# Second feed-forward block of a macaron layer: first feature block computed directly, token sums in place on VectorE, modulation on ScalarE, a buffer of its own for the second weight unit

## Chip, cores and metric

The kernel runs on one core of a Trainium2 chip. The metric is the device time of one execution in microseconds; times below are of this kernel on that one core, and the profile is of one execution.

## The reference, cut to what matters

One layer on 1024 latent tokens of width 1024 (and a context of 256): a feed-forward block, a mixer, a second feed-forward block, a last norm. The change touches the second feed-forward block alone.

```python
def rmsnorm(x, g):
    y = x * lax.rsqrt(jnp.mean(x * x, axis=-1, keepdims=True) + EPS)
    return y * g

def modulate(h, shift, scale):
    return h * (1 + scale) + shift

def swiglu(h, w1, w2):                       # w1: 1024 x 5632, w2: 2816 x 1024
    gate, up = jnp.split(h @ w1, 2, axis=-1)
    return (jax.nn.silu(gate) * up) @ w2

...
x = x + m_x[5] * (jnp.concatenate([ret_x, gm_x], axis=-1) @ w_out[l])      # the mixer's output projection
x = x + 0.5 * m_x[8] * swiglu(modulate(rmsnorm(x, norm_g[l, 2]), m_x[6], m_x[7]), ffn2_w1[l], ffn2_w2[l])
return rmsnorm(x, final_g)
```

## The kernel before

Everything lies transposed: features on the 128 partitions, tokens along the free axis, in two halves of TB = 512 tokens. Each float32 product is made of three matmuls on split operands: a *high* part (ScalarE copies the float32 tile to float32r) and a *low* part (tile minus high, on GpSimd or VectorE); high x high, high x low, low x high (`mm3`, L1449 to L1451, and `product`, L1702 to L1704).

The five engines each have a program written out by hand, in order; semaphores join them. Nothing schedules them: what stands ahead in an engine's program runs first. SyncE issues all loads.

**The second feed-forward block** goes through NF = 22 feature blocks of 128 hidden features, with two units of weights each: `block_unit(g)`, 1 MB into WR slot 0 (gate and up columns, 1024 x 256), and `down_unit(g)`, 0.5 MB into W2R. The product of a feature block's weights with all tokens is a 2x2 block product (feature rows 0 to 511 and 512 to 1023, by gate and up, by the token halves), computed by Strassen's scheme in its form by Winograd with NM = 7 products instead of 8. It needs sums of weight blocks (`weight_sums`: four VectorE subtractions and additions, L1193 to L1199, one of them in place in WR) and four sums of token blocks, made once: V0 = B12 - B11, V1 = B22 - V0, V2 = B22 - B12, V3 = B21 - V1, where B11, B21 are the modulated tiles of the first token half and B12, B22 those of the second. The product m of block g waits for the low part of its weights and adds up in PSUM (`product_bank`); ScalarE copies three of the banks to SBUF (PU, U2, U3: `first_copy`, `second_copy`, `third_copy`), VectorE adds the other bank to them, ScalarE takes SiLU, VectorE multiplies, and the result is split into PXH and PXL. The down projection (`down`, 8 output tiles for each token half, 48 matmuls) goes through four PSUM banks, from which VectorE adds into X (L1355). It runs one block late: the down projection of block g-1 stands between the products of block g. `block_period` is one such period on each engine; the last 20 periods are a loop and its tail.

**The order around the change.** The mixer's output projection ends with eight fills of 24 matmuls for the second token half (`("out", 1, b)`). Meanwhile VectorE adds them into X (L1302), ScalarE squares (L657), VectorE adds the squares (L920) and makes the weight sums of block 0; ScalarE and GpSimd split the weights of block 0 (`weight_high`, L720, `weight_low`, L597). TensorE then runs products 0 and 1 of blocks 0 and 1, which need only the first token half, with the two norm steps of the second half in between (`norm_sum`, L1459; `norm_scale`, L1469). For the second half, VectorE does for each k of four: two scalings by the norm factor (`scaled`, L948, into B12 and B22), two modulations (`modulated`, L955), V0 and V1 (L1389, L1392). ScalarE makes the high parts (`token_high`, L746), GpSimd the low parts of V1, V2 and V3 (`token_low`, L608), VectorE those of V0 and of B22 itself (L1397, L1406). V0 and V2 share one buffer, V1 and V3 another (VT0, VT1). So block 0 has its products 2 to 6 behind those token sums; block 1's weights go through the same WR slot as block 0's and are loaded when block 0's low parts are done.

## Time and profile before

| | |
|---|---|
| runs | 2225.57, 2230.71, 2232.66 us; median 2230.71 |
| profiled execution | 2225.84 us, of which the span from first to last instruction is 2224.0 |
| mean granted TensorE clock | 0.984 of full speed |
| TensorE / VectorE / GpSimd / ScalarE busy | 96% / 59% / 30% / 24% of the span |
| end of the mixer's output projection | 1488.0 us |
| start of the first down projection of the second feed-forward block | 1557.2 us |
| one period of the loop behind it | 30.1 us |

Rows are read like this: a row of a timeline gives start and length in us, the engine, the line of the kernel, the operation with output<-inputs, and in brackets how long the engine stood idle before it and who released it. A row of groups gives count, busy time, the mean in ns and the idle time before. PE is TensorE, DVE VectorE, ACT ScalarE, POOL GpSimd, SPq SyncE's queue. A matmul of 512 columns shows 0.39 us but the next one starts 0.23 us after it: they overlap.

### The profile page before, as it was taken

What the parts mean: (1) busy time and instruction counts of PE and PEld (TensorE: products, weight loads), DVE (VectorE), ACT (ScalarE), POOL (GpSimd) and SP (SyncE); (2) the same over time, 40 slices, a digit from 0 to 9 for tenths busy, and PEclk for the clock granted to TensorE, in tenths of its full rate; (3) what the DMA queues carried; (4) which work ended last, traced back from release to release, by engine and by line L of the source; (5) the groups of instructions that cost most, each with busy time, mean ns of one, the idle gap of its engine ahead of it and who ended that gap; (6) DMA issues with size and microseconds to landing.
All of it is one profiled execution on the core that took longest, in us unless ns stands there. A gap on an engine that the chain in (4) does not pass through costs nothing.

```text
span 2224.0 us, 28807 instructions
## 1 busy us (share of the span) xinstructions
PE 2142.8 (96%) x10884; PEld 1793.8 (81%) x10884; DVE 1320.5 (59%) x2012; ACT 539.5 (24%) x812; POOL 664.3 (30%) x349
## 2 busy tenths in 40 slices
PE   7999999999999999998999999995999999999995
PEld 3688888888888888887888898874888888888884
DVE  4654454454454454469644444478777777777767
ACT  3312111111111111124221222334222323223222
POOL 1611111111111111126232232565343443343430
PEclk9999999999999999999999999997999999999997
DMA  9212112112111111113101021210101111111112
GB/s 343 76 48 94 54 40 85 56 47 74 67 47 67 74 47 66 76 38 120 57 20 38 20 88 55 76 67 29 57 30 54 57 57 57 57 39 46 57 38 76
DMA packets 28376, 144.41 MB, mean 65 GB/s; under 512 B 3360, under 2 KB 4640, under 8 KB 15008
## 3 DMA queue, kind: packets, MB, share of 16 engines
q1 hardware_dynamic: 28320, 143.64, 17.4%
q8 instruction: 38, 0.62, 0.1%
q14 instruction: 18, 0.15, 0.0%
HBM read 139.44 MB, written 4.19 MB: 65 GB/s over the span
## 4 chain that ended last, share of the span: by engine, by line
PE 87%; DVE 6%; issue 2%; DMA 2%; POOL 1%; ACT 1%; SPq 0%; DVEq 0%; ACTq 0%; POOLq 0%
PE PS L1449 22%; PE PS L1451 21%; PE PS L1450 21%; PE PS L1702 6%; PE PS L1703 6%; PE PS L1704 6%; PE PS L1495 1%; DVE ACC L920 1%; PE PS L1486 1%; POOL HL L510 1%; DMA WR<-w_units 1%; DMA X<-x 1%; PE PS L1644 1%; DVE B L955 1%; DVE HF L955 1%
## 5 line engine op out<-in xcount | busy, mean ns | idle before, releaser
L1449 PE MATMUL PS<-HH,WH 128*128 128x512 f32 x1088 | 427.0, 393 | 3.7 <-POOL HL L510 3.0
L1450 PE MATMUL PS<-HL,WH 128*128 128x512 f32 x1088 | 424.1, 390 | 0.0
L1451 PE MATMUL PS<-HH,WL 128*128 128x512 f32 x1088 | 423.9, 390 | 0.0
L493 POOL TENSOR_TENSOR WL<-WR,WH 128x2048 fp32r<-128x2048 f32 x42 | 193.3, 4603 | 535.1 <-ACT WH L643 534.9
L1355 DVE SCALAR_TENSOR_TENSOR X<-PS,GATE,X 128x512 f32<-128x512 f32 x352 | 242.9, 745 | 93.6 <-PE PS L1451 93.6
L1449 PEld LDWEIGHTS PS<-HH,WH 128*128 128x128 f32 x1088 | 204.7, 188 | 46.6 <-issue 4.1
L1451 PEld LDWEIGHTS PS<-HH,WL 128*128 128x128 f32 x1088 | 204.7, 188 | 42.9
L1450 PEld LDWEIGHTS PS<-HL,WH 128*128 128x128 f32 x1088 | 204.8, 188 | 41.8 <-issue 0.7
L1078 DVE TENSOR_TENSOR PR<-SG,PS 128x512 f32<-128x512 f32 (+1 forms) x66 | 39.5, 599 | 296.8 <-ACT SG L695 291.5
L597 POOL TENSOR_TENSOR WVL<-WR,WVH 128x512 fp32r<-128x512 f32 x88 | 124.4, 1424 | 255.0 <-ACT WVH L720 255.0
L1094 DVE SCALAR_TENSOR_TENSOR X<-PS,GATE,X 128x512 f32<-128x512 f32 x176 | 132.1, 751 | 108.0 <-PE PS L1451 108.0
L695 ACT ACTIVATE SG<-PS 128x512 f32<-128x512 f32 (+1 forms) x66 | 34.5, 523 | 641.3 <-PE PS L1451 641.2
L1449 PE MATMUL PS<-PH,W2H 128*128 128x512 f32 (+1 forms) x528 | 188.4, 357 | 0.6 <-DVE X L1094 0.6
L1451 PE MATMUL PS<-PH,W2L 128*128 128x512 f32 (+1 forms) x528 | 187.0, 354 | 0.0
L1450 PE MATMUL PS<-PL,W2H 128*128 128x512 f32 (+1 forms) x528 | 186.8, 354 | 0.0
L526 POOL TENSOR_TENSOR W2L<-W2R,W2H 128x1024 fp32r<-128x1024 f32 x22 | 53.6, 2438 | 375.1 <-ACT W2H L704 375.1
L1054 DVE SCALAR_TENSOR_TENSOR AS<-WR,CS,AS 128x256 f32<-128x256 f32 x336 | 156.4, 539 | 0.0
L1449 PE MATMUL PS<-PXH,W2H 128*128 128x512 f32 x352 | 140.1, 398 | 2.8 <-DVE PXL L1349 1.4
L1702 PE MATMUL PS<-HH,WVH 128*128 128x512 f32 x352 | 139.7, 397 | 2.1 <-POOL WVL L597 1.4
L1703 PE MATMUL PS<-HL,WVH 128*128 128x512 f32 x352 | 139.2, 396 | 0.0
L1451 PE MATMUL PS<-PXH,W2L 128*128 128x512 f32 x352 | 138.6, 394 | 0.0
L1704 PE MATMUL PS<-HH,WVL 128*128 128x512 f32 x352 | 138.1, 392 | 0.0
...
## 6 DMA issues: line engine op xcount, KB each, us to landing
...
```

The source lines that it names most:

```text
L493: pool.tensor_tensor(WL[:, slot], WR[:, slot], WH[:, slot].bitcast(F32), ALU.subtract).then_inc(s_lo[slot], 1)
L526: pool.tensor_tensor(w2l[:, j], w2r[:, :], w2h[:, j].bitcast(F32), ALU.subtract).then_inc(s_w2lo, 1)
L597: pool.tensor_tensor(WVL[:, m], weight_block(m), WVH[:, m].bitcast(F32), ALU.subtract).then_inc(s_wl, 1)
L1054: ins = dve.scalar_tensor_tensor(dst, w, c, dst, ALU.mult, ALU.add)
L1094: dve.scalar_tensor_tensor(xv, PS[down_bank(s, k)][:, 0:nt], GATE[:, 0, k, s:s + 1], xv, ALU.mult, ALU.add).then_inc(s_yd, 1)
L1355: dve.scalar_tensor_tensor(xv, y_bank(n)[:, :], GATE[:, 2, d, 0:1], xv, ALU.mult, ALU.add).then_inc(s_fyd, 1)
L1449: pe.matmul(dst, wh, xh, start=first, stop=False)
L1450: pe.matmul(dst, wh, xl, start=False, stop=False)
L1451: return pe.matmul(dst, wl, xh, start=False, stop=last)
L1702: pe.matmul(bank[:, :], wh, xh, start=first, stop=False, skip_group_check=True)
L1703: pe.matmul(bank[:, :], wh, xl, start=False, stop=False, skip_group_check=True)
L1704: ins = pe.matmul(bank[:, :], wl, xh, start=False, stop=k == 3, skip_group_check=True)
```

## The change

1. **Block 0 is computed directly**: gate and up of each token half as plain sums over all eight feature tiles, 4 x 24 matmuls (`direct`), so that it needs no token sums and no weight sums. Its gate and up land in banks of their own (0 and 1 for the first half, 2 and 3 for the second); VectorE multiplies SiLU(gate) by up straight out of PSUM. Products 2 to 6 of block 1 are now the first that need token sums.
2. **Weights of block 1** have a buffer of their own, RAW1, loaded once the mixer's inputs are done; the weight sums ahead of the norm are those of block 1. Their parts go to seven slots in another order (`SLOT1`), since block 0 takes four.
3. **Token sums in place** in B11, B12, B21, B22 (V0 in B11, V1 in B22, V2 in B12, V3 in B21); all their low parts are made by VectorE. GpSimd makes the low parts of B12 instead (`norm_low`).
4. **Modulation** of the second half is one ScalarE instruction (`second_modulated`, a scale and a bias per partition) instead of VectorE's.
5. TensorE runs, after the output projection: direct first half (48 matmuls, with the norm steps between), products 0 and 1 of block 1, direct second half (48), products 2 and 3 of block 1, down projection of block 0's first half, product 4, second half, products 5 and 6. Then the loop, unchanged, from block 2 on.

```diff
@@ TensorE @@
+            def direct(bank, t, n, done=None, ready=None, base=0):
+                slot, half = DIRECT[n], n % 2
+                cols = slice(t * TB, (t + 1) * TB)
+                pe.wait_ge(s_wl, n + 1)
+                for k in range(4):
+                    if ready is not None:
+                        pe.wait_ge(ready, base + k + 1)
+                    ins = mm3(PS[bank][:, :], WVH[:, slot, k, :], WVL[:, slot, k, :], HH[:, 4 * half + k, cols],
+                              HL[:, 4 * half + k, cols], half == 0 and k == 0, half == 1 and k == 3)
...
-            product(0, 0, 0)
+            direct(A0, 0, 0, s_m[0])
             norm_sum(2, 2)
-            product(0, 0, 1)
+            direct(A0, 0, 1, s_m[1])
             norm_scale(2, 2)
+            direct(B_, 0, 2)
+            direct(B_, 0, 3, s_m[5])
             product(1, 1, 0)
-            pe.wait_ge(s_c11, 1)
+            pe.wait_ge(s_g1, 1)
             product(1, 1, 1)
...
+            direct(2, 1, 0, s_m[2], s_hl, 8 * J[2, 2])
+            direct(3, 1, 2, s_m[4])
+            direct(2, 1, 1, s_m[6], s_bl)
+            direct(3, 1, 3, s_m[3])
+            pe.wait_ge(s_p1, 1)
+            product(1, 1, 2, s_vl[1])
...
+            product(1, 1, 3, s_vl[0])
+            pe.wait_ge(s_fp[1], 1)
             pe.wait_ge(s_fyd, NYB)
-            block_period(0, 0, first=True)
-            block_period(1, 1, second=True)
+            down(0, 0)
+            pe.wait_ge(s_u2, 1)
+            product(1, 1, 4, s_vl[2])
+            down(0, 1)
+            pe.wait_ge(s_u3, 1)
+            product(1, 1, 5, s_vl[3])
+            pe.wait_ge(s_c22, 1)
+            product(1, 1, 6)
@@ VectorE @@
+            for k in range(KT):
+                scaled(2, 2, k)
...
+                dve.tensor_tensor(B11[:, k, :], B12[:, k, :], B11[:, k, :], ALU.subtract).then_inc(s_v[0], 1)
...
+            dve.tensor_tensor(PU[:, 0, :], SG1[:, :], PS[A0][:, :], ALU.mult).then_inc(s_fp[0], 1)
...
+            for k in range(4):
+                dve.wait_ge(s_v[3], k + 1)
+                token_low(1, k)
+            for k in range(4):
+                token_low(0, k)
...
+            for d in range(KT):
+                down(0, 0, d)
+                if d % 2:
+                    token_low(3, d // 2)
             up_first(1, 1)
+            next_sums(2)
+            for d in range(KT):
+                down(0, 1, d)
+                if d == 1:
+                    gate_second(1)
@@ ScalarE @@
+            def second_modulated(k):
+                j, h = J[2, 2], modulated_tile(2, 2, k)
+                act.wait_ge(s_xm, 8 * j + k + 1)
+                act.activation(h, h, ACT.Identity, scale=GAIN[:, 2, k, 0:1], bias=MODS[:, 6 * KT + k, 0:1]).then_inc(s_hf, 1)
@@ GpSimd @@
+            for n, slot in enumerate(DIRECT):
+                low_part(slot, weight_block(slot), n + 1)
+            for m in range(3):
+                weight_low(1, m, RAW1)
             norm_rsqrt(2, 2)
-            weight_low(1, 0)
-            weight_low(1, 1)
-            for v in (1, 2, 3):
-                for k in range(4):
-                    token_low(v, k)
-            block_period(0, first=True)
-            block_period(1)
+            norm_low(2, 2, 0, 4)
+            for m in range(3, NM):
+                weight_low(1, m, RAW1)
+            down_low(0)
+            for m in range(6):
+                weight_low(2, m)
+            down_low(1)
@@ SyncE @@
+            sp.wait_ge(s_cat, 16)
+            sp.dma_start(RAW1[:, :, :], w_units[U_FFN2 + 1]).then_inc(s_raw1, 16)
...
-            block_unit(1)
-            with sp.Fori(1, NF - 1) as g:
+            block_unit(2)
+            sp.wait_ge(s_dl, 1)
+            down_unit(1)
+            with sp.Fori(2, NF - 1) as g:
```

**VectorE's order, before**: the last of the four rounds on the second half and what follows (X is the residual, PS4 the bank with the norm factor, VT0 and VT1 the buffers of the sums, L1323 the addition into PU).

```order
L948 TENSOR_TENSOR B12_147<-X_49,PS4 128x512
L948 TENSOR_TENSOR B22_148<-X_49,PS4 128x512
L955 TENSOR_SCALAR B12_147<-B12_147,GAIN_57,MODS_55 128x512 [waits scaled_done]
L955 TENSOR_SCALAR B22_148<-B22_148,GAIN_57,MODS_55 128x512 [waits scaled_done]
L1389 TENSOR_TENSOR VT0_139<-B12_147,B11_145 128x512 [waits modulated_done]
L1392 TENSOR_TENSOR VT1_140<-B22_148,VT0_139 128x512 [waits token_sum0_ready,modulated_done]
L1323 TENSOR_TENSOR PU_134<-PU_134,PS1 128x512 [waits first_product_copied,product1_ready]
L1397 TENSOR_TENSOR HL_51<-VT0_139,HH_50 128x512 [waits token_sum0_high_done]
L1400 TENSOR_TENSOR VT0_139<-B22_148,B12_147 128x512 [waits token_sum1_ready,token_sum0_low_done]
```

**VectorE's order, changed**, the same place: the scalings stand together, the modulations are gone, the gated multiply (L1458) and block 6's low part (L1462) stand ahead of the sums, and the low parts of V1 and V0 (L1446) come after all sums.

```order
L1011 TENSOR_TENSOR B12_142<-X_49,PS4 128x512 x3
L1011 TENSOR_TENSOR B22_144<-X_49,PS4 128x512 x4
L1455 TENSOR_TENSOR B11_141<-B12_142,B11_141 128x512 [waits modulated_done,modulated_low_done]
L1455 TENSOR_TENSOR B11_141<-B12_142,B11_141 128x512 [waits modulated_done] x3
L1458 TENSOR_TENSOR PU_134<-SG1_128,PS0 128x512 [waits product1_ready,silu_first_half_done]
L1462 TENSOR_TENSOR HL_51<-B22_144,HH_50 128x512 [waits modulated_high_done] x4
L1466 TENSOR_TENSOR B12_142<-B22_144,B12_142 128x512 [waits token_sum0_ready,modulated_low_done] x4
L1470 TENSOR_TENSOR B22_144<-B22_144,B11_141 128x512 [waits last_block_low_done,token_sum2_ready] x4
L1418 TENSOR_TENSOR PXL_133<-PU_134,PXH_132 128x512 [waits gated_high_done0]
L1474 TENSOR_TENSOR B21_143<-B21_143,B22_144 128x512 [waits token_sum1_ready] x4
L1446 TENSOR_TENSOR V2L_146<-B22_144,V2H_145 128x512 [waits token_sum1_high_done,token_sum3_ready] x4
```

Behind the eleven rows come the low parts of V0 and V2 and the first additions of the down projection; before, the sums of each k stood right behind its modulation.

**ScalarE's order, before**, around the first SiLU of the block (G2, SG1):

```order
L737 ACTIVATE U3_131<-PS0 128x512 [waits product4_ready]
L720 ACTIVATE WVH_141<-ST_127 128x512 [waits weight_sums_ready,block_unit_loaded,product2_ready]
L720 ACTIVATE WVH_141<-WR_52 128x512 [waits weight_sums_ready,block_unit_loaded,product3_ready]
L720 ACTIVATE WVH_141<-ST_127 128x512 [waits weight_sums_ready,block_unit_loaded,product4_ready]
L770 ACT_TABLE_LOAD
L770 ACTIVATE G2_135<-G2_135 128x512 [waits gate_second_half_ready]
L774 ACTIVATE SG1_128<-PS0 128x512 [waits product5_ready]
L720 ACTIVATE WVH_141<-WR_52 128x512 [waits block_unit_loaded,product5_ready]
```

**ScalarE's order, changed**, from the norm high parts of the second half on; SG1 is the SiLU of block 0's first half, V2H the high part of sum V1.

```order
L678 ACTIVATE HH_50<-B12_142 128x512 [waits modulated_done] x4
L772 ACT_TABLE_LOAD
L772 ACTIVATE SG1_128<-PS1 128x512 [waits product5_ready]
L894 ACTIVATE B22_144<-B22_144,MODS_55,GAIN_57 128x512 [waits scaled_done] x4
L678 ACTIVATE HH_50<-B22_144 128x512 [waits modulated_done] x4
L749 ACTIVATE PU_134<-PS7 128x512 [waits product0_ready]
L762 ACTIVATE PXH_132<-PU_134 128x512 [waits gated_ready0]
L776 ACTIVATE W2H_137<-W2R_129 128x1024 [waits down_unit_loaded]
L731 ACTIVATE WVH_139<-RAW1_151 128x512 [waits weight_sums_ready,product2_ready]
L731 ACTIVATE WVH_139<-ST_127 128x512 [waits weight_sums_ready,product4_ready]
L766 ACTIVATE V2H_145<-B22_144 128x512 [waits token_sum1_ready] x4
L766 ACTIVATE HH_50<-B11_141 128x512 [waits token_sum0_ready] x4
```

The table load and the first SiLU moved up between the two groups of modulations (L894), and the high parts of the token sums (L766) stand behind two weight parts that wait for products of the direct block.

**GpSimd's order, before**, from the norm's reciprocal root on (VXL: low parts of token sums):

```order
L499 TENSOR_TENSOR RS_66<-MS_65,NEGH_67 128x4 [waits norm_mean_ready]
L597 TENSOR_TENSOR WVL_142<-WR_52,WVH_141 128x512 [waits weight_block_high_done] x2
L608 TENSOR_TENSOR VXL_144<-VT1_140,VXH_143 128x512 [waits token_sum1_high_done] x4
L608 TENSOR_TENSOR VXL_144<-VT0_139,VXH_143 128x512 [waits token_sum2_high_done] x4
L608 TENSOR_TENSOR VXL_144<-VT1_140,VXH_143 128x512 [waits last_block_low_done,token_sum3_high_done] x4
L597 TENSOR_TENSOR WVL_142<-ST_127,WVH_141 128x512 [waits weight_block_high_done]
L597 TENSOR_TENSOR WVL_142<-WR_52,WVH_141 128x512 [waits weight_block_high_done]
```

**GpSimd's order, changed**, from the same place (RAW1: block 1's own unit):

```order
L518 TENSOR_TENSOR RS_66<-MS_65,NEGH_67 128x4 [waits norm_mean_ready]
L529 TENSOR_TENSOR HL_51<-B12_142,HH_50 128x512 [waits modulated_high_done] x4
L616 TENSOR_TENSOR WVL_140<-RAW1_151,WVH_139 128x512 [waits weight_block_high_done]
L616 TENSOR_TENSOR WVL_140<-ST_127,WVH_139 128x512 [waits weight_block_high_done]
L616 TENSOR_TENSOR WVL_140<-RAW1_151,WVH_139 128x512 [waits weight_block_high_done]
L616 TENSOR_TENSOR WVL_140<-ST_127,WVH_139 128x512 [waits weight_block_high_done]
L623 TENSOR_TENSOR W2L_138<-W2R_129,W2H_137 128x1024 [waits down_unit_high_done]
L616 TENSOR_TENSOR WVL_140<-WR_52,WVH_139 128x512 [waits weight_block_high_done] x2
```

Twelve low parts of token sums left the engine, four of B12 came, and the weight parts of block 1 and W2L follow at once.

## Rows read from the trace of the kernel before

**Rows 1.** Page, part 2: busy tenths of TensorE in 40 slices of the span

```profile
PE   7999999999999999998999999995999999999995
```

**Rows 2.** Stretches: us, length, busy us per engine (x instructions), PEclk, DMA

```profile
1503.20:1517.40 14.20, 5.05 (x13) 2.96 (x13) 13.82 (x21) 3.45 (x6) 4.15 (x3) 0.68 0.00 1
...
1526.40:1532.30 5.90, 0.01 (x1) 0.01 (x1) 5.90 (x6) 2.37 (x4) 4.43 (x3) 0.71 0.00 0
...
1552.70:1573.60 20.90, 20.86 (x85) 17.05 (x85) 16.59 (x22) 5.60 (x9) 8.58 (x7) 0.92 0.00 1
...
1573.60:1603.70 30.10, 30.10 (x132) 24.59 (x131) 22.61 (x28) 8.95 (x15) 12.00 (x9) 1.00 0.14 53
```

**Rows 3.** Waits, 1480 to 1580 us: who for whom, total, times, longest

```profile
PE PS L1702 <- POOL VXL L608: 9.9, 4, 3.2
...
PE PS L1702 <- ACT U L733: 6.3, 1, 6.3
...
PE PS L1702 <- ACT U L737: 5.9, 1, 5.9
...
PE PS L1702 <- POOL WVL L597: 1.4, 1, 1.4
```

**Rows 4.** Groups, TensorE, 1603 to 2130 us: count, busy us, mean ns, idle before

```profile
L1702 PE MATMUL PS<-VXH,WVH 128*128 128x512 f32 x209 | 82.0, 392 | 0.3 <-ACT U L733 0.3
```

**Rows 5.** Timeline, TensorE: start, length (us), line, output<-inputs, [idle before <-releaser]

```profile
1491.37 1.05 PE L1459 MATMUL PS<-ONES,ACC 128*128 128x1 f32 x8 [0.47 <-DVE ACC L920]
...
1495.13 1.02 PE L1469 MATMUL PS<-DG,ONES 128*128 128x512 f32 x2
...
1603.93 0.40 PE L1702 MATMUL PS<-HH,WVH 128*128 128x512 f32 x1
```

**Rows 6.** Timeline, VectorE, around the norm of the second half

```profile
1488.20 0.75 DVE L1302 SCALAR_TENSOR_TENSOR X<-PS,GATE,X 128x512 f32<-128x512 f32 x1 [4.09 <-PE PS L1451]
...
1496.19 1.29 DVE L948 TENSOR_TENSOR B<-X,PS 128x512 f32<-128x512 f32 x2 [0.17 <-PE PS L1469]
```

**Rows 7.** Timeline, VectorE and GpSimd, single rows between 1496 and 1575 us

```profile
1558.07 5.51 DVE L1355 SCALAR_TENSOR_TENSOR X<-PS,GATE,X 128x512 f32<-128x512 f32 x8 [2.06 <-PE PS L1451]
...
1572.66 2.48 DVE L1349 TENSOR_TENSOR PXL<-PU,PXH 128x512 fp32r<-128x512 f32 x1
...
1496.20 2.55 POOL L597 TENSOR_TENSOR WVL<-WR,WVH 128x512 fp32r<-128x512 f32 x2 [2.49 <-ACT WVH L720]
...
1572.19 2.41 POOL L601 TENSOR_TENSOR W2L<-W2R,W2H 128x1024 fp32r<-128x1024 f32 x1 [4.13 <-ACT W2H L780]
```

**Rows 8.** Timeline of ScalarE; then its groups: count, busy us, mean ns, idle

```profile
1481.03 1.14 ACT L720 ACTIVATE WVH<-WR 128x512 fp32r<-128x512 f32 x2
...
L770 ACT ACT_TABLE_LOAD x1 | 1.3, 1283 | 0.0
...
L831 ACT ACTIVATE KZ<-PS,Z 128x512 f32<-128x512 f32 x16 | 9.7, 698 | 0.0
```

**Rows 9.** Timeline, GpSimd and VectorE side by side, 1518 to 1526 us

```profile
1518.84 6.53 POOL L608 TENSOR_TENSOR VXL<-VT,VXH 128x512 fp32r<-128x512 f32 x4 [2.93 <-ACT VXH L746]
...
1520.85 1.67 DVE L1400 TENSOR_TENSOR VT<-B,B 128x512 f32<-128x512 f32 x1
1522.44 1.79 DVE L1403 TENSOR_TENSOR VT<-B,VT 128x512 f32<-128x512 f32 x1
```

**Rows 10.** Timeline, SyncE's queue and VectorE: a load and its first reader

```profile
1545.81 0.34 SPq L456 DMA_DIRECT2D WR<-w_units  x1
...
1551.06 0.69 DVE L1193 TENSOR_TENSOR ST<-WR 128x512 f32<-128x512 f32 x1 [3.82 <-DMA WR<-w_units]
```

**Rows 11.** Timeline, TensorE, start-up of the second feed-forward block

```profile
1511.48 0.79 PE L1702 MATMUL PS<-VXH,WVH 128*128 128x512 f32 x1 [3.19 <-POOL VXL L608]
...
1520.82 0.63 PE L1704 MATMUL PS<-HH,WVL 128*128 128x512 f32 x1
1521.25 0.63 PE L1702 MATMUL PS<-HH,WVH 128*128 128x512 f32 x1
```

366 lines of the change are left out of this document (204 added, 162 removed).

## Prediction

> **What bounds the kernel now.** The page comes first: TensorE's row of tenths stands at 9 nearly everywhere and has one dip away from the two ends, a 5 in slice 28, which begins at 27 x 55.6 = 1501 us [rows 1]. The table of stretches opens that dip. From 1573.7 us on, one feature block takes 30.10 us, TensorE is busy throughout, and 132 matmuls went by, 0.228 us each, at a granted clock of 1.00. From 1503.2 to 1517.4 it passes 13 matmuls in 14.2 us at a clock of 0.68, and from 1526.4 to 1532.3 one [rows 2]. The waits of the stretch name what it stood for: 9.9 us for GpSimd's low parts of the token sums (L608) and once each 6.3 and 5.9 us for ScalarE's copies U2 and U3 [rows 3]. The time to win is therefore the start-up of the second feed-forward block, between the last output projection (1488.0) and the steady loop; the loop itself has no idle TensorE time (0.3 us in 527 us) [rows 4] and its code is unchanged.
>
> Call the mark "end of block 2" the last matmul of product 6 of the third feature block, at 1603.9 in the trace (the first matmul after it starts at 1603.93) [rows 5]. Everything behind it runs at TensorE's pace, so the kernel gains what this mark moves.
>
> **TensorE's own work.** Before the mark it does 132 x 3 less one projection of 48, so 348 matmuls; the direct block has 2 x 2 x 8 x 3 = 96 instead of 84, so 360 afterwards: 12 x 0.228 = +2.7 us. With 360 x 0.228 = 82.1 us and 2.5 us for the two norm steps (0.47 of waiting and 1.05, then 1.0) [rows 5] the mark could not come before 1488.0 + 84.6 = 1572.6. The bound of the gain is 31.3 us. The rest of the sum is how much of it the new waits keep.
>
> **Durations taken.** VectorE on 128x512: 0.60 us start to start (two take 1.28) [rows 6], 0.68 for an addition into X (eight take 5.51) [rows 7]. ScalarE 0.52 start to start (two take 1.14) [rows 8]; GpSimd 1.26 (two take 2.55), and 2.41 for W2L [rows 7]. What one engine writes is taken up by the next within 0.1 us.
>
> **VectorE and GpSimd get in each other's way.** While GpSimd works through four low parts without a pause (6.53 us, 1.63 each), VectorE's subtractions show 1.67 and 1.79 instead of 0.68 [rows 9], and so I charge 1.0 us to a VectorE instruction with two SBUF operands that finds GpSimd running, and 2.1 us against W2L from its start (half a microsecond later, a subtraction took 2.48 there) [rows 7]. Instructions that read PSUM are not charged (the scalings and the additions into X, [rows 6, 7]). The change puts all sixteen low parts of the token sums on VectorE, twelve more than now, while GpSimd splits weights beside it, so this decides the sum. The Trainium skill, page "SBUF — State Buffer", section "Who interferes with whom", puts it harder: the pair of ports is locked for the whole instruction and the second one blocks fully. By the letter of that, an alternating pair would cost 1.29 + 0.68 = 1.97 us; the trace has 1.63. The row is used; the rule's reading is a rival below.
>
> **The chain after the change.** *1488.0 to 1517.9.* TensorE has 96 direct matmuls and products 0 and 1 of block 1 (24), 27.4 us, and the norm steps, with no wait. Its weights are there: the four direct parts stand two fills earlier in ScalarE's queue than now, and block 1's unit has a buffer of its own, loaded while the mixer's output is projected, so that the wait for a weight low part ahead of block 1 (1.4 us) goes [rows 3]. The scale row is ready at 1496.2 as now, VectorE scales eight tiles to 1501.0, ScalarE modulates behind it. For this ScalarE step on 128x512 no row exists: a plain copy takes 0.62 (1.14 less 0.52), a scaled one from PSUM 0.70 [rows 8]; either leaves it 0.8 us or less away from where it is counted and off the path, I take 0.70. The table load for SiLU (1.28 [rows 8]) now stands before product 1: SG1 is ready near 1503.6, TensorE asks at 1504.3, so it costs nothing, with 0.7 us of cover. The low parts of the second half's first tiles are there by 1506, asked at 1507.0; those of the last four by 1509.5, asked at 1512.4.
>
> *1517.9 to 1526.7: the first new wait.* Product 2 needs the low parts of token sum 1. VectorE's order is: 8 scalings (1501.0), 4 sums V0 of which three meet GpSimd's norm low parts (+3, 1506.4), the gated multiply, 4 low parts of block 6 (1509.4), 4 sums V2 and 4 sums V1, one meeting GpSimd each (+2, 1516.3), one low part, 4 sums V3 (1519.3). Then come the four low parts wanted; they meet weight low parts 5 and 6 and then W2L (+1.0, +1.0, +2.1), because ScalarE hands those over just then: finished at 1520.0, 1521.6, 1523.2 and 1525.9. TensorE waits 2.2 + 0.8 + 0.8 + 1.9 = 5.7 us and is through product 2 at 1526.7, through product 3 at 1529.5.
>
> *To 1536.7: projection of block 0, first half.* VectorE still has 4 low parts, a multiply, 4 low parts and one more before its first addition at 1531.8; its 8 additions carry 4 low parts between them. With four PSUM banks TensorE's fifth and seventh pieces wait: 0.4 + 1.2 = 1.6 us. Product 4 ends at 1539.5.
>
> *To 1553.5: second half.* VectorE now does the addition into PU and four weight sums (0.73 each, dependent) ahead of the additions: the fifth piece waits to 1544.5, 2.3 us, another 0.5 behind it. Products 5 and 6 end at 1553.5.
>
> *Block 2.* Products 0 to 3 end at 1564.6. Product 4 needs U2, which stands on ScalarE behind the first weight part of block 3, and that behind its load. SyncE issues the load only after W2L of block 1 (POOL: five weight parts and W2L after 1551.6, so 1561.7). In the trace its first reader starts 5.25 us after its issue (1545.81 to 1551.06) [rows 10]; so 1567.3, two highs and a copy, 1569.1: a wait of 4.5 us, where the trace of before has 6.3 [rows 3]. The remaining 84 matmuls end at 1588.4.
>
> **Sum.** 1603.9 - 1588.4 = 15.5 us earlier. Against it stands the clock. In the trace the matmuls went 0.43 us apart (the 1.2 GHz level) after the interrupted stretch, from 1511.5 to 1521.6, then 0.23 again (2.4 GHz) [rows 11]; after the wait of 6.3 us it was eight matmuls, 8 x 0.2 = 1.6 us. I charge 1.6 us behind the wait of 4.5 us, and 1.0 us for product 3, most of whose delay the projection's waits absorb. Gain: 15.5 - 2.6 = 12.9, taken as 13 us. Nothing else is charged: VectorE's and GpSimd's collisions before 1488 (four lows against the weight sums, up to 4 us) fall into VectorE's 4.1 us of idle time before 1488.2 [rows 6]; if that cover fails, the norm step slips by as much, 2 us for 2.
>
> The profiled execution took 2225.84 us (span 2224.0): 2212.8. The three runs have their median at 2230.71, 4.9 us above it, so the forecast is put at 2217.7, 2217.5 rounded.
>
> **Rivals.**
> *Harder collisions or a slower clock (2222).* If GpSimd and VectorE exclude each other for whole instructions (1.29 and 0.68), the first wait becomes about 10 us instead of 5.7 and the mark 1595.1: gain 8.8. If instead the low clock level lasts from product 2 to the end of the first half projection (36 matmuls more at +0.2 = 7 us, less absorbed waits), the mark is 1595.5: gain 8.4. For: the trace kept the low level for 22 matmuls after an interrupted stretch much like the new one. Against: GpSimd's instructions alternate at 1.63 [rows 9].
> *No collisions (2207).* If VectorE's order falls between GpSimd's instructions, all the charges (7 us and what follows from them) go: mark 1579.5, gain 24. Against: both engines are fed by the same ScalarE queue in turn.
> *The new order is ScalarE's problem; the change gives little (2228).* Behind its waits for products 2 and 4 (L731) stand the token highs; if each of the in-order steps slips by what the modulations and the table load add (8 x 0.1 + 1.3) at the three places where TensorE waits already, and the norm step slips by 4 us from the uncovered collisions, some 10 us go: gain 3.
> *Slower.* One mechanism: the clock. The new start has waits of 0.4 to 4.5 us spread over 1518 to 1569. If they keep TensorE at 1.2 GHz from product 2 on, its 156 matmuls up to block 2's product 4 take 0.427 each; the waits vanish behind them, product 4 starts at 1588.7 and the mark is 1609.8, 6 us later than now; if it lasts through block 2, 1624.6, +21 us, 2251. It decides from block 2's product 4 on; below it the change is not slower. Against: in the trace dense work was granted the full clock again each time, as from 1552.7 on (0.92, then 1.00) [rows 2].
>
> **Chances.** Forecast 0.64, its own range 2212 to 2222; harder collisions or clock 0.17; none 0.09; little 0.06; slower 0.04. A measurement of this kernel tells about 0.3%, 6.7 us, from no change. The forecast counts as faster but for its tail, the second case for two thirds, the third wholly: faster 0.79, within 0.3% 0.17, slower 0.04. The range 2208 to 2226 leaves out most of "none", half of "little" and "slower", and allows for the 3.5 us by which the runs differ.
>
> **What would show it.** Right: direct matmuls from 1488 to 1518 with no wait; then a wait on VectorE's V2L lasting 5 to 7 us in pieces at product 2; waits on X additions of 1 to 3 us in each half projection; one wait on U2 of 4 to 5 us in block 2; VectorE subtractions of 1.7 us beside GpSimd's. Block 2 ends near 1591. Wrong: a wait on SG1 or on a low part of HL before 1518; no wait at product 2; a granted clock under 0.8 after 1530; a period other than 30.1 us in the loop.

## Result and profile after

The changed kernel takes 2218.25 us (median of 5 runs, 2215.21 to 2220.49); the kernel before took 2228.82 in the same comparison (5 runs, 2225.57 to 2232.66). The ratio is 0.995 with a 95% interval of 0.9937 to 0.9964, so 10.6 us are gained (8.0 to 14.0 by the interval), where 13 were forecast. Three executions of the kernels below, or of the kernel before beside them, took 3584 to 6221 us and are left out of every median. The profiled execution took 2215.21 us with a span of 2213.4; before it was 2225.84 and 2224.0.

The page of the changed kernel, part 2, TensorE's tenths and its granted clock:

```profile
PE   8899999999999999998999999998899999999995
...
PEclk9999999999999999999999999999999999999998
```

The 5 in slice 28 [rows 1] is gone; two 8s stand in slices 28 and 29. The stretches show what is left (start:end, length, TensorE's busy us and matmuls, clock, DMA):

```profile
1503.20:1518.00 14.80, 14.80 (x66) 1.00 0.00 1
1518.00:1527.00 9.00, 5.80 (x23) 0.95 0.00 1
1527.00:1540.00 13.00, 9.42 (x31) 0.77 0.13 42
1540.00:1555.00 15.00, 13.45 (x58) 1.00 0.00 0
1555.00:1570.00 15.00, 12.29 (x53) 1.00 0.28 103
1570.00:1590.00 20.00, 16.80 (x65) 0.83 0.01 2
1590.00:1620.10 30.10, 30.10 (x133) 1.00 0.14 53
```

From 1503 to 1518 TensorE has no gap, where it had passed 13 matmuls in 14.2 us [rows 2]. Three places remain: 1518 to 1527, 1527 to 1540, 1570 to 1590. The waits from 1480 to 1580 us name them:

```profile
PE PS L1789 <- ACT U L753: 5.7, 1, 5.7
...
PE PS L1536 <- POOL W2L L623: 3.6, 1, 3.6
...
PE PS L1789 <- issue: 2.3, 1, 2.3
PE PS L1536 <- DVE X L1424: 1.6, 2, 1.3
...
PE PS L1789 <- DVE V2L L1446: 0.9, 1, 0.9
...
PE PS L1546 <- DVE ACC L983: 0.6, 1, 0.6
```

The 9.9, 6.3, 5.9 and 1.4 us of [rows 3] have become 5.7, 3.6, 2.3, 1.6 and 0.9. The same waits in TensorE's timeline, and the mark:

```profile
1491.90 0.27 PE L1546 MATMUL PS<-ONES,ACC 128*128 128x1 f32 x1 [0.59 <-DVE ACC L983]
...
1519.56 0.47 PE L1789 MATMUL PS<-V2H,WVH 128*128 128x512 f32 x1 [0.88 <-DVE V2L L1446]
...
1524.86 0.47 PE L1789 MATMUL PS<-HH,WVH 128*128 128x512 f32 x1 [2.32 <-issue]
...
1532.86 0.70 PE L1536 MATMUL PS<-PXH,W2H 128*128 128x512 f32 x1 [3.58 <-POOL W2L L623]
...
1573.20 0.79 PE L1789 MATMUL PS<-V3H,WVH 128*128 128x512 f32 x1 [5.66 <-ACT U L753]
...
1594.38 0.39 PE L1789 MATMUL PS<-HH,WVH 128*128 128x512 f32 x1
```

**The length of the start-up** is used from here on: from the first matmul of the norm sum to the first behind the mark. It was 1491.37 to 1603.93 [rows 5], 112.6 us; now it is 1491.90 to 1594.38, 102.5 us, for twelve matmuls more. Counting TensorE's matmuls from start to start splits it: at 0.229 us each they need 79.2 us before and 82.0 now; gaps over 0.5 us add 27.6 and 16.4; matmuls 0.33 to 0.5 us apart (36 and 26 of them) add 6.3 and 4.9, of which 28 and 23, with 5.4 and 4.6 us, go at about 0.43 us, the slow clock level, and the rest are single ones 0.34 us apart behind a wait; rounding takes 0.6 and 0.8 off. So the start-up gains 10.1 us: 11.2 of gaps and 1.4 of these matmuls, less 2.7 for more work. It begins 0.5 us later, and from the mark to the end of the span it took 620.1 us before and 619.0 here. That 1.1 us is no part of the change: the eleven kernels of the table below have the same loop but for the exchanged loads, and ten of their traces show 619.0 to 620.7 there, one (GpSimd asks later) 613.8. So the 10.6 us of span are 10.1 of start-up and 1.1 behind it, less the 0.5 ahead.

**Where the low parts got stuck.** Product 3 (1524.86) is put down to "issue", but it begins as GpSimd's weight low part of its slot ends. GpSimd's timeline (start, length, [idle before]):

```profile
1511.87 12.89 POOL L616 TENSOR_TENSOR WVL<-RAW,WVH 128x512 fp32r<-128x512 f32 x1 [4.45 <-ACT WVH L731]
1524.72 1.75 POOL L616 TENSOR_TENSOR WVL<-ST,WVH 128x512 fp32r<-128x512 f32 x1
...
1529.81 2.79 POOL L623 TENSOR_TENSOR W2L<-W2R,W2H 128x1024 fp32r<-128x1024 f32 x1
```

An instruction of 1.3 us took 12.89. VectorE meanwhile:

```profile
1501.51 6.46 DVE L1455 TENSOR_TENSOR B<-B,B 128x512 f32<-128x512 f32 x4
...
1510.90 2.49 DVE L1466 TENSOR_TENSOR B<-B,B 128x512 f32<-128x512 f32 x4
1513.31 2.49 DVE L1470 TENSOR_TENSOR B<-B,B 128x512 f32<-128x512 f32 x4
...
1518.72 2.50 DVE L1446 TENSOR_TENSOR V2L<-B,V2H 128x512 fp32r<-128x512 f32 x4
1521.13 2.50 DVE L1446 TENSOR_TENSOR HL<-B,HH 128x512 fp32r<-128x512 f32 x4
1523.54 0.69 DVE L1482 TENSOR_TENSOR UP<-G,PS 128x512 f32<-128x512 f32 x1
1524.13 6.26 DVE L1446 TENSOR_TENSOR V3L<-B,V3H 128x512 fp32r<-128x512 f32 x4
```

Nineteen VectorE instructions with two SBUF operands start 0.60 us apart while GpSimd's stands (the last at 1522.93); then one with an operand in PSUM (L1482) comes, and GpSimd is done 1.2 us after its start. Ahead of that, and behind it, the two alternate: four take 6.46 and 6.26 us, 1.6 each, as in [rows 9].

### The profile page after: what moved, and what is told of

Same layout as the page of the kernel before. It is cut to its first block, busy times and chain, and to the rows that moved or that the text cites. A ratio compares the mean times of both kernels' runs of the same rounds, so it can differ in the third digit from the quotient of the medians.

```text
span 2213.4 us, 28764 instructions
## 1 busy us (share of the span) xinstructions
PE 2140.8 (97%) x10896; PEld 1792.3 (81%) x10896; DVE 1315.8 (59%) x2009; ACT 544.0 (25%) x818; POOL 665.6 (30%) x338
## 4 chain that ended last, share of the span: by engine, by line
PE 88%; DVE 5%; POOL 2%; DMA 1%; issue 1%; ACT 1%; SPq 0%; DVEq 0%; POOLq 0%; ACTq 0%
PE PS L1536 22%; PE PS L1538 22%; PE PS L1537 21%; PE PS L1789 6%; PE PS L1790 6%; PE PS L1791 6%; PE PS L1582 2%; POOL WVL L616 1%; DMA WS<-ada_units 1%; PE PS L1573 1%; POOL HL L529 1%; PE PS L1731 1%; DVE DG L996 1%; DVE ACC L983 1%; DMA WR<-w_units 1%
## 5 line engine op out<-in xcount | busy, mean ns | idle before, releaser
L1537 PE MATMUL PS<-PXL,W2H 128*128 128x512 f32 x352 | 138.8, 394 | 0.0
L1789 PE MATMUL PS<-HH,WVH 128*128 128x512 f32 x336 | 132.4, 394 | 2.3 <-issue 2.3
L1790 PE MATMUL PS<-HL,WVH 128*128 128x512 f32 x336 | 132.3, 394 | 0.0
```

The costliest lines, as they stand in the source:

```text
L1537: pe.matmul(dst, wh, xl, start=False, stop=False)
L1789: pe.matmul(bank[:, :], wh, xh, start=first, stop=False, skip_group_check=True)
L1790: pe.matmul(bank[:, :], wh, xl, start=False, stop=False, skip_group_check=True)
```

## Experiments

All ratios and gains are to the kernel before as it ran beside each kernel: median 2228.82 us beside the changed one; 2227.11 beside "pauses", "second weights early" and "loads exchanged"; 2228.64 beside "one pause", "both" and the exchange in the kernel before; 2229.23 beside the last three. The gain is the difference of the two medians. Since the changed kernel ran beside none of the others, gains are compared here and not medians. "Start-up" is the length defined above, in the profiled execution, one of each kernel.

| kernel | median us | gain us | ratio, 95% | start-up us |
|---|---|---|---|---|
| before | 2228.82 | | | 112.6 |
| changed | 2218.25 | 10.6 | 0.995 (0.9937 to 0.9964) | 102.5 |
| loads exchanged, in the kernel before | 2223.32 | 5.3 | 0.9971 (0.996 to 0.9983) | 108.9 |
| pauses in VectorE | 2218.18 | 8.9 | 0.996 (0.9948 to 0.9972) | 103.8 |
| one pause | 2217.31 | 11.3 | 0.9943 (0.9926 to 0.996) | 102.5 |
| second weights early | 2214.60 | 12.5 | 0.9945 (0.9933 to 0.9958) | 101.1 |
| loads exchanged | 2209.65 | 17.5 | 0.9925 (0.9911 to 0.9939) | 96.1 |
| both | 2211.72 | 16.9 | 0.9914 (0.9897 to 0.9931) | 95.2 |
| GpSimd asks later | 2215.45 | 13.8 | 0.9941 (0.9922 to 0.9959) | 101.4 |
| modulation on VectorE | 2217.60 | 11.6 | 0.995 (0.9938 to 0.9963) | 104.8 |
| V1's low parts on GpSimd | 2218.25 | 11.0 | 0.9953 (0.994 to 0.9965) | 105.9 |

No run undoes the direct block, the buffer RAW1 or the sums in place by themselves. That the direct block and the buffer fill the hole from 1503 to 1518 is read from the waits that are gone there; how the gain divides between them was not tested.

### Pauses in VectorE's run

Does VectorE's unbroken run keep GpSimd out? Each of its sums V2, V1 and V3 and of the low parts of V0, V1 and V2 waits for the one before it; the wait is met by the program's order and leaves only a gap.

```diff
+                dve.wait_ge(s_v[2], k)          # ahead of V2's k-th sum; the like for V1, V3 and the low parts of V0, V1, V2
```

> The changed kernel with one kind of wait more: each of VectorE's sums V2, V1, V3 and each low part of the token sums waits for the one before it on VectorE (already done in order, so only a gap arises). Theory A: the weight low part that GpSimd shows with 12.89 us comes down to 3.5 us or less, product 3 no longer waits 2.3 us for it, and W2L is ready some 5 to 8 us earlier, so the 3.58 us ahead of the first half projection go; in exchange VectorE's subtractions show 1.6 to 1.7 us where GpSimd is at work, and product 2 waits 3 to 6 us on the token low parts instead of 0.9: the time within 3 us of the changed kernel's 2218, ratio to before 0.993 to 0.997. Theory B/C (VectorE's order is not what holds GpSimd): the 12.89 us stay over 8, the waits of products 2 and 3 and of the projection stay as they are.

GpSimd's timeline in that kernel:

```profile
1513.61 1.68 POOL L616 TENSOR_TENSOR WVL<-RAW,WVH 128x512 fp32r<-128x512 f32 x1 [4.45 <-ACT WVH L731]
1515.69 1.32 POOL L616 TENSOR_TENSOR WVL<-ST,WVH 128x512 fp32r<-128x512 f32 x1 [0.39 <-ACT WVH L731]
1523.99 1.38 POOL L616 TENSOR_TENSOR WVL<-RAW,WVH 128x512 fp32r<-128x512 f32 x1 [6.98 <-ACT WVH L731]
1525.33 1.73 POOL L616 TENSOR_TENSOR WVL<-ST,WVH 128x512 fp32r<-128x512 f32 x1
1527.01 2.81 POOL L623 TENSOR_TENSOR W2L<-W2R,W2H 128x1024 fp32r<-128x1024 f32 x1
```

The same instruction takes 1.68 us, and the waits for it and for W2L are gone. The bill goes to VectorE: product 2 now waits 5.6 and 1.1 us for V2L. The start-up is 1.3 us longer; the gain, 8.9 us, can't be told from the changed kernel's 10.6 (the intervals overlap). Shown: to be held off was not dear, for with the other engine slowed TensorE waits for about the same sum (6.7 us from product 2 to the projection's first half, 6.8 in the changed kernel). Not shown by this run: that the pauses let GpSimd in, since they also moved its asking, from 0.37 to 0.16 us behind the start of a VectorE instruction.

### The two engines by themselves

> A kernel by itself, with none of the reference's work: three phases, each run twice, of twelve VectorE subtractions on 128x512 (two SBUF operands) beside four GpSimd ones that may start when VectorE's second has ended. In 'plain' nothing stands between VectorE's twelve; in 'waits' each waits for the one before; in 'psum3' nothing waits, and every fourth reads an operand from PSUM. Theory A (an unbroken run of VectorE instructions with two SBUF operands keeps GpSimd out, and VectorE itself is not slowed): plain, VectorE twelve in 7.2 to 7.6 us, GpSimd's first shown with 5.5 to 7 us, its others 1.2 to 1.3; waits, the two alternate, VectorE about 1.6 to 1.7 apart while GpSimd has work (four of them), so twelve in 11 to 12 us; psum3, GpSimd gets in at VectorE's 4th, 8th and 12th. Theory B, the prediction's (VectorE is charged 1.0 us for each one that finds GpSimd running, whatever stands between them): VectorE takes 11 us in plain and waits alike, and GpSimd's last 1.6 each. Theory C (the long GpSimd instruction waited for its operand, no port is involved): GpSimd 1.2 to 1.3 each and VectorE 0.6 each in all phases.

Here GpSimd was never kept out, in any phase. The first phase, without waits, in the timelines of GpSimd (its four instructions) and VectorE (its fourth):

```profile
7.50 6.65 POOL L60 TENSOR_TENSOR PP<-C,E 128x512 f32<-128x512 f32 x4 [7.06 <-DVE DD L52]
...
7.94 1.75 DVE L52 TENSOR_TENSOR DD<-A,B 128x512 f32<-128x512 f32 x1
```

GpSimd's four take 6.65 us, 1.66 each, and VectorE's fourth and following 1.75 until GpSimd has finished, whether VectorE's instructions wait for one another or not. That is what the prediction had charged (about 1.0 us for each). So "an unbroken run keeps GpSimd out" is not the whole condition; as a general rule it falls. In the big kernels GpSimd had asked at different moments of a VectorE instruction, and up to then the losers had asked late in it. So the moment of asking was varied:

```python
act.activation(F[:, :width], C[:, :width], Copy).then_inc(s_a, 1)     # lets GpSimd go; width sets the moment
```

> A kernel by itself, with none of the reference's work: twelve phases, in each sixteen VectorE subtractions on 128x512 with two SBUF operands, back to back, and two GpSimd ones that are let go by a ScalarE copy started when VectorE's second ends; the copy's width goes through 16, 112, 208, 304, 400 and 496 elements, so that GpSimd asks at six different points of a VectorE instruction (pitch 0.60 us). In the second six phases each VectorE instruction has a wait, met long ago, ahead of it. Theory A (unbroken VectorE instructions always keep GpSimd out) has fallen in the kernel before this one, where GpSimd got in at the first boundary. Theory D: it depends on where GpSimd asks. In the traces it asked 0.15, 0.16 and 0.31 us behind the start of a VectorE instruction and was done 1.5 to 1.7 us later, and at 0.37 and 0.40 us and was kept out for 12.9 and 5.6 us, until VectorE read PSUM. So: phases in which it asks up to about 0.33 us behind a start show its first instruction with 1.4 to 1.8 us and alternation from there; phases in which it asks later than that show it with 5 us or more, to the end of the sixteen. Theory E (waits ahead of the VectorE instructions make the difference): the first six phases alike at 1.4 to 1.8, the second six alike and long. Theory F (neither, something of the big kernel): all twelve 1.3 to 1.9.

GpSimd got in each time, its first instruction in 1.31 to 1.84 us, with and without waits ahead of VectorE's. The moments between 0.21 and 0.41 us behind a start had been left out, and those were the ones that lost in the big kernels:

> A kernel by itself, with none of the reference's work: ten phases of sixteen VectorE subtractions (two SBUF operands, back to back, 0.60 us apart) and two GpSimd ones let go by a ScalarE copy, whose width goes from 520 to 736 elements in steps of 24, so that GpSimd asks between about 0.23 and 0.42 us behind the start of a VectorE instruction, in steps of 0.02 us. The run before it had asked at 0.05, 0.13, 0.21, 0.41, 0.49 and 0.57 us and got in each time within 1.3 to 1.8 us. In the traces of the big kernels GpSimd was kept out when it had asked at 0.35, 0.37, 0.37, 0.40 and 0.41 us, and got in at 0.14, 0.22, 0.30, 0.42, 0.44 and 0.47. Theory D2 (a narrow window of asking points loses, wherever the kernel): the phases between about 0.33 and 0.40 show GpSimd's first instruction with 5 us or more, until the sixteen are over, the others 1.3 to 1.8. Rival G (the window is chance, and something else of the big kernel keeps GpSimd out): all ten phases at 1.3 to 1.8.

All ten phases got in; asked at 0.35 us behind a start, GpSimd's pair took

```profile
79.88 3.12 POOL L71 TENSOR_TENSOR PP<-C,E 128x512 f32<-128x512 f32 x2 [8.77 <-ACT F L63]
```

1.46 and 1.71 us. The window falls too.

### Asking later, in the real kernel

```diff
+            pool.wait_ge(s_wh, weights_done(1, 3))
+            for n in range(2):
+                pool.memset(NUDGE[:, n, :], 0.0)
```

> The changed kernel with two tiny GpSimd writes (8 columns each, of a buffer that nobody reads) ahead of its weight low part of product 3, behind the same wait: GpSimd asks 0.1 to 0.4 us later, at another point of VectorE's run, and nothing else changes. Theory D2 (it is the asking point): the instruction that took 12.89 us takes 1.3 to 1.9, the next ones alternate with VectorE, whose V1 and V3 sums and V2L slip by 1 to 3 us in all; product 2 waits 2 to 4 us instead of 0.9, product 3 not at all, the first projection less than 3.6: the same 2216 to 2219 in total, since one wait takes the place of another. Rival G (VectorE's unbroken run in this kernel keeps GpSimd out wherever it asks): 10 to 13 us again, and the waits as they were.

```profile
1514.43 0.14 POOL L641 MEMSET NUDGE<- 128x8 f32 x2 [4.41 <-ACT WVH L735]
1514.53 1.40 POOL L617 TENSOR_TENSOR WVL<-RAW,WVH 128x512 fp32r<-128x512 f32 x1
1516.41 1.82 POOL L617 TENSOR_TENSOR WVL<-ST,WVH 128x512 fp32r<-128x512 f32 x1 [0.48 <-ACT WVH L735]
1523.93 5.65 POOL L617 TENSOR_TENSOR WVL<-RAW,WVH 128x512 fp32r<-128x512 f32 x1 [5.70 <-ACT WVH L735]
```

Asked 0.42 instead of 0.37 us behind the start of a VectorE instruction (0.10 us behind the two small writes), the instruction of 12.89 us takes 1.40, with VectorE's run as unbroken as before; two instructions on, another is kept out for 5.65. So it is no property of the kernel, nor of the instruction: each asking is won or lost. Won askings cost VectorE, and product 2 waits 3.3 us instead of 0.9, product 3 not at all, the projection 2.6; the start-up is 1.1 us shorter. All askings of GpSimd, after idle time, into an unbroken two-operand run in the start-ups with the change, worked out from the starts in the timelines (us behind the start of VectorE's instruction, then what GpSimd's took):

| kernel | kept out | got in |
|---|---|---|
| changed | 0.37: 12.89 | |
| loads exchanged | 0.37: 12.89 | |
| one pause | 0.35: 10.51 | 0.52: 1.33 |
| second weights early | 0.40: 5.63 | 0.30: 1.54; 0.14: 1.70 |
| both | 0.41: 5.65 | 0.30: 1.54; 0.14: 1.71; 0.47: 1.38 |
| asks later | 0.41: 5.65 | 0.42: 1.40; 0.01: 1.82 |
| modulation on VectorE | 0.48: 13.98 | |
| V1's low parts on GpSimd | 0.22: 5.20 | 0.35: 1.48; 0.14: 1.71 |

No window of moments separates the two columns: 0.48 and 0.22 lost, 0.47, 0.14 and 0.35 won. What decides an asking stays open. What ended each of the eight is the same: VectorE's next instruction that read PSUM, or a pause.

### One pause

> The changed kernel with a single wait more: ahead of VectorE's low parts of token sum 0 it waits for its own low parts of token sum 1. Theory (a pause of VectorE lets GpSimd in): GpSimd's held instruction ends near 1522.3 in place of 1524.8, product 3 no longer waits 2.3 us (0 to 0.6), GpSimd's parts 4 to 6 and W2L come 1 to 2.5 us earlier and the 3.6 us wait ahead of the first half projection shrinks to 1 to 3; VectorE loses 1.1 us at the place and perhaps three more of these behind it, which nobody waits for until the additions into X. Gain against the changed kernel's 2218: 2 to 4 us, 2214 to 2216, ratio to before 0.993 to 0.995. Rival (GpSimd gets in, but VectorE's slower run takes the place of the wait, as in the kernel with all the pauses): 2217 to 2219, with the projection held by PXL or X instead.

One wait, ahead of the low parts of token sum 0, and up to it everything as in the changed kernel:

```profile
1512.91 10.51 POOL L616 TENSOR_TENSOR WVL<-RAW,WVH 128x512 fp32r<-128x512 f32 x1 [4.43 <-ACT WVH L731]
```

GpSimd's held instruction ended at 1523.4, 1.1 us behind the pause (VectorE's next instruction starts at 1522.30) and after 10.51 us instead of 12.89: here the pause did let it in. But then it alternated with VectorE's four low parts; product 3 waited 0.6, 0.7, 0.7 and 0.7 us piece by piece on those instead of 2.3 once, the projection 1.5 twice. Start-up 102.5 us, as without, and the median within the rival's 2217 to 2219: the waits of this stretch are dealt out differently, and their sum stays.

### Second weights of block 0 early

```diff
             square(2, 2, 7)
+            down_high(0)
...
             norm_rsqrt(2, 2)
+            down_low(0)
             norm_low(2, 2, 0, 4)
```

> The changed kernel with block 0's second weights split early: ScalarE's copy right behind the last norm's last square, GpSimd's low part right behind the norm step and ahead of the norm's low parts. Theory A: GpSimd being held off by VectorE cost the first half projection its 3.58 us of waiting (on W2L); that goes or falls below 1.0, and TensorE is then held there by nothing or by the additions into X for 0.5 to 1.5; product 3's 2.3 us stay; the norm's low parts slip by 0 to 1 us. Gain against the changed kernel 1.5 to 3 us (part of the wait was the clock's anyway): 2215 to 2217, ratio to before 0.993 to 0.995. Rival (the wait stands for the low clock or for VectorE's additions, which come in its place): the same 2218, a wait of over 3 us on X or PS instead. A second rival: the GpSimd low part of 2.4 us ahead of the norm's pushes SG1 and the first low parts past TensorE's demand: slower, 2220 or more.

This takes 2.4 us of GpSimd out of the crowded stretch into one where it idles. The waits from 1480 to 1590 us:

```profile
PE PS L1789 <- ACT U L753: 5.7, 1, 5.7
PE PS L1789 <- DVE V2L L1446: 3.1, 1, 3.1
PE PS L1536 <- DVE X L1424: 1.9, 2, 1.7
PE PS L1556 <- DVE DG L996: 1.4, 1, 1.4
```

The 3.6 us for W2L are gone and so are product 3's 2.3; 3.1 for V2L (2.2 more than before) and 1.4 at the norm step came. The latter is the encounter of [rows 9] again: VectorE's instruction ahead of the norm step runs beside GpSimd's W2L (1492.14 to 1494.53) and takes 2.87 us, where it takes 0.69 in the changed kernel:

```profile
1492.21 2.87 DVE L996 TENSOR_TENSOR DG<-ID,RS 128x512 f32<-128x512 f32 x1 [1.12 <-POOL RS L518]
```

The start-up is 1.4 us shorter, just under the theory's 1.5 to 3, but product 3's wait, which the theory left standing, went too. By the medians the gain is 12.5 us instead of 10.6, and the intervals overlap.

### The two loads of SyncE's round exchanged

```diff
             with sp.Fori(2, NF - 1) as g:
-                sp.wait_ge(s_dl, g)
-                down_unit(g)
                 sp.wait_ge(s_wl, weights_done(g, 5))
                 block_unit(g + 1)
+                sp.wait_ge(s_dl, g)
+                down_unit(g)
```

> The changed kernel with two loads of each round of SyncE's loop exchanged: the weights of the next block ahead of the second weights. Theory A (the 5.7 us wait of block 2's product 4 on U2 comes from the load that SyncE issues only once W2L of block 1 is done, at 1564.7): the load goes out at the latest when GpSimd has the fifth weight part, 2.5 to 3 us earlier, so the wait falls to 2.5 to 3.5 us, its low clock stretch of 10 matmuls shortens, and the kernel gains 2.5 to 4 us: 2214 to 2216, ratio 0.992 to 0.994. Rival (the bandwidth or ScalarE's order holds U2, not the issue): the wait stays at 5 to 6 us and the time at 2218. Second rival: the second weights come later in the steady loop and TensorE waits there: a new wait on W2H or W2L each block of 0.3 us or more, slower by 4 us or more.

The issues on SyncE's queue, first of the changed kernel, then of this one:

```profile
1532.63 32.45 SPq L474 DMA_DIRECT2D W2R<-w_units  x2
1565.37 0.34 SPq L471 DMA_DIRECT2D WR<-w_units  x1
```

```profile
1532.49 0.33 SPq L474 DMA_DIRECT2D W2R<-w_units  x1
1561.85 0.34 SPq L471 DMA_DIRECT2D WR<-w_units  x1
1564.66 0.34 SPq L474 DMA_DIRECT2D W2R<-w_units  x1
```

The unit of block 3 goes out 3.5 us sooner, and TensorE's wait and what follows it read:

```profile
1568.53 0.49 PE L1789 MATMUL PS<-V3H,WVH 128*128 128x512 f32 x1 [1.01 <-ACT U L753]
```

```profile
1570.00:1590.00 20.00, 20.00 (x89) 1.00 0.16 53
```

The wait falls from 5.66 to 1.01 us, and with so short a one the clock stays at full speed: the eight matmuls 0.43 us apart behind the long wait are gone, 8 x 0.2 = 1.6 us. 4.65 + 1.6 = 6.25 of the 6.4 us by which the start-up is shorter. Forecast were 2.5 to 4 us: the mechanism was right, the size too small. Of the 4.65 us, 3.5 are the earlier issue and 1.2 a shorter load: 4.9 us from the issue to the first reader (1561.85 to 1566.77) instead of 6.1, now that no load of second weights goes out just ahead of it; whether that is why was not tested. By the medians the gain is 17.5 us instead of 10.6. The loop behind it has no new wait.

> Block 0's second weights split early, and the loads exchanged, together. Alone, the first took the 3.58 us wait away and gave about 3.7 us, the second took 4.6 us from the wait of block 2's product 4 with its slow stretch and gave about 8.6 us. If they act at different places they add up: 2205 to 2208, ratio to before 0.990 to 0.992, with no wait on W2L in the start-up and at most 1.2 us on U2. Rival (what one wins the other's wait absorbs, since both move product 4 of block 2 against the same load): no more than the exchange alone, 2209 to 2211, and the wait on U2 back at 3 us or more.

Together: start-up 95.2 us, W2L and product 3 not waited for, 3.1 us on V2L, 3.6 on the additions into X, 1.6 on U2. It is 0.8 us shorter than with the loads exchanged alone, and the ratios cannot tell the two apart (0.9914 and 0.9925 with overlapping intervals): the two gains do not add up, as forecast, though the wait on U2 did not come back to 3 us either, which the rival asked for. The interval of the kernel with both lies wholly below the changed kernel's; that of the exchange alone touches it (0.9939 and 0.9937). The likeliest reading, not tested, is that VectorE, which the early second weights do not relieve, ends the waits last.

### The same exchange in the kernel before

> The kernel before with the same two loads exchanged and nothing else. The wait of 6.3 us on U2 in block 2 was there before the change too. If SyncE's order made it, it shrinks by 4 to 5 us with the slow matmuls behind it and the kernel gains 5 to 8 us: 2219 to 2223, ratio 0.996 to 0.998: two thirds of what the whole change gives. Rival (in the kernel before the wait was the second weights' or ScalarE's): 2226 to 2228, the wait still 5 us or more. In the loop behind, the period stays 30.1 us by either.

```profile
1549.72 0.79 PE L1702 MATMUL PS<-VXH,WVH 128*128 128x512 f32 x1 [2.42 <-ACT U L733]
```

6.31 us [rows 3] become 2.42, the start-up is 3.6 us shorter, the median 5.3 lower (4 to 9 by the ratio's interval): the cause as forecast, the gain at the lower end. So the exchange is worth about half as much as the whole change without touching a single computing engine, and more in the changed kernel, where it also spares the slow clock: here six matmuls still go 0.43 us apart behind the 2.42 us.

### Two parts of the change undone

> The changed kernel with one part of the change undone: the second half's modulation goes back to VectorE, each right behind the scaling of the next tile. VectorE gets eight instructions of 0.53 to 0.60 us more in the one stretch in which all wait for it, 4.2 to 4.8 us; ScalarE is rid of eight at 0.73. If VectorE's order sets the start-up: V0 sums and all behind them 3 to 4.8 us later, product 2 waits 4 to 6 us instead of 0.9, part of which product 3's and the projection's waits take up; 2 to 4 us slower than the changed kernel: 2220 to 2222, ratio to before 0.996 to 0.998. Rival (the modulation's place is of no matter, what counts is ScalarE's or GpSimd's): within 1 us of 2218. Second rival (the high parts come sooner without the modulations and the table load, and pull everything forward): 2215.

The rival holds by the medians: a gain of 11.6 us, no difference from 10.6. In the profiled executions the start-up is 2.3 us longer, with 1.7 us on V2L and 5.0 on W2L; one GpSimd instruction was kept out for 13.98 us. Whether the modulation's place is worth 0 or 2 us stays unsettled; it is at most a small part of the gain.

> The changed kernel with the four low parts of token sum 1 on GpSimd (behind its weight parts 3 and 4) and no longer on VectorE: the share of the work as nearer to the kernel before. If GpSimd is kept out as in the changed kernel (it asks at 1511.9, VectorE reads PSUM 2.4 us sooner, near 1521.1), its parts 3 and 4 end at 1524 and the four low parts at 1530.5: product 2 waits 10 to 12 us, product 3 and the projection's W2L wait goes partly into it; 5 to 9 us slower than the changed kernel: 2223 to 2227, ratio 0.997 to 1.000. If GpSimd gets in at once because its asking point has moved, weight parts 3 and 4 end by 1516, the low parts by 1523: product 2 waits 4 to 5 us: 2219 to 2221. Rival (VectorE is the bound and freeing it of 2.4 us pays): under 2216.

GpSimd's timeline:

```profile
1513.82 1.48 POOL L616 TENSOR_TENSOR WVL<-RAW,WVH 128x512 fp32r<-128x512 f32 x1 [4.43 <-ACT WVH L738]
1515.91 1.71 POOL L616 TENSOR_TENSOR WVL<-ST,WVH 128x512 fp32r<-128x512 f32 x1 [0.61 <-ACT WVH L738]
1521.32 10.26 POOL L644 TENSOR_TENSOR V2L<-B,V2H 128x512 fp32r<-128x512 f32 x4 [3.70 <-DVE B L1481]
```

GpSimd got in at its two weight parts, as in the second case, and was then kept out at the first low part. Product 2 waits 6.0 us at once instead of 4 to 5. The start-up is 3.4 us longer; the median is the changed kernel's to the digit, 2218.25 (0.9953, 0.994 to 0.9965), and no case had that. GpSimd takes 1.3 us for what VectorE does in 0.6, so the low parts come late on it; part of it is made good, since product 3 then doesn't wait at all and the projection 2.15 us for W2L.

## Why the prediction was right, and where not

**The bound and the direct block: right.** From 1496 to 1518 TensorE stands nowhere: norm steps, direct products, SG1 (ready at 1504.4, no wait), low parts, block 1's weights from their own buffer. VectorE's sums and GpSimd's lows before 1488 did collide (1.68 us each of the four), and the idle 4.1 us took it up as stated; the norm sum came 0.5 us later, well within the 1489.8 to 1496.4 at which it comes in the kernels of the table.

**Product 2: the step that failed.** "They meet weight low parts 5 and 6 and then W2L (+1.0, +1.0, +2.1)", with two more charges at the sums, had V2L's last part at 1525.9 and TensorE waiting 5.7 us. It was there at 1521.2, and TensorE waited 0.9. The charge of 1.0 us for each VectorE instruction that finds GpSimd waiting was read from [rows 9], where the two alternate. V0's sums bore it (6.46 us for four, 1.0 each, where three were charged), the nineteen behind bore none, since GpSimd was not let in. The Trainium skill, page "SBUF — State Buffer", section "Who interferes with whom", says that issue order decides who is blocked and that the blocked one stops fully; here GpSimd's instruction stopped fully, not for one instruction of VectorE but for nineteen. Neither the rule nor the row foretold that.

**What was not charged took its place.** If GpSimd pays, its products come late: product 3 waited 2.3 us for a weight part and the first projection 3.6 us for W2L, where the prediction had 1.6 for the additions into X and nothing for W2L. Predicted waits from product 2 to the projection's first half 7.3 us, measured 6.8. So the sum came out for a reason that the prediction did not have, and that it came out so closely is in part luck. Not wholly: with V2L slowed as predicted (the pauses) product 2 waits 5.6 and 1.1 us, the other two waits vanish, and the sum is 6.7. But with the same work dealt out in other ways it was 5.9 (GpSimd asks later), 8.1 (loads exchanged, which up to there is the same program), 8.2 (V1's low parts on GpSimd) and 9.0 us (modulation on VectorE).

**Second half of the projection:** 2.8 us predicted, 1.3 and 0.3 measured. **Block 2's wait:** 4.5 predicted, 5.66 measured, cause right (the exchange of the loads shows it): the load was issued at 1565.4 rather than 1562, as GpSimd was late with W2L of block 1 (1561.70 to 1564.55), and it took 6.1 us from issue to its first reader (1565.37 to 1571.44) instead of 5.25. TensorE asked 3 us later too.

**The clock, the term that was too small:** 2.6 us charged, behind product 3 and block 2's wait; the matmuls at the slow level took 4.6 us more than at full speed, 5.4 before the change. The eight behind the wait for W2L were not charged, for the prediction had no wait there. Part of them was free: in the changed kernel six of product 3's went at the slow level, and the wait for W2L behind was 3.6 us; in the kernel with the loads exchanged none did, and it was 5.0. Slow matmuls ahead of a fixed arrival shorten the wait by what they cost.

**The sum:** the start-up was to last 1591.0 - 1491.4 = 99.6 us and lasted 102.5. The waits come to 0.9 + 2.3 + 3.6 + 1.3 + 0.3 + 0.3 + 5.7 = 14.2 us (14.6 predicted), the slow matmuls to 4.6 (2.6 predicted); another 1.3 us are that the first matmul behind a wait is followed later than 0.23 us, by up to 0.6, which the prediction put at nothing. The terms of the sum that were mis-sized are therefore the clock, by 2.0 us, and this restart; together with 0.4 less of waiting they make the 2.9 us by which the start-up was longer than forecast.

**The gain and the time.** 10.6 us were measured and 13 forecast, which the runs alone can't tell apart (8.0 to 14.0). That the time, 2218.25, lies within 0.8 us of the forecast 2217.5 is luck in part: the forecast put the median of the kernel before 4.9 us above its profiled execution, from three runs, and five gave 3.0; the missing 2.4 us of gain and the 1.9 us by which that median fell nearly cancel.

**By its own signs** it was right on the stretch up to 1518, on a wait for V2L coming next, on VectorE's 1.7 us beside GpSimd and on the loop. The wait at product 2 was 0.9 and not 5 to 7 us, that on U2 5.7 and not 4 to 5, and one sign of being wrong was nearly there: "a granted clock under 0.8 after 1530" stood on that list, and it was 0.77 from 1527 to 1540 and 0.83 from 1530 to 1540.

**Slips in its figures**, none of which moves the forecast. The low level behind the interrupted stretch of [rows 11] lasted 17 matmuls (three from 1511.48, fourteen from 1515.96), not 22. The charges of its chain up to V2L add up to 3 + 2 + 4.1 = 9.1 us, where the case without collisions speaks of 7. In the slower case 1588.7 plus 84 matmuls of 0.228 is 1607.9, not 1609.8, unless some of them are slow.

**Rivals.** Harder collisions: no, an instruction of VectorE was slowed by 1.1 us, against W2L by 2.1, as charged. The slower clock of the same case: no, the low level held for six and eight matmuls in this stretch, where that case had 36. No collisions: half true, for VectorE alone. ScalarE as the bound: no, only U2 waits behind it, for a load. Slower by the clock: no; dense work got the full clock back each time, at 1536.3 and 1577.2.
